# Two handovers of an expert layer moved across stage boundaries: the first gathers of routed rows, the gathers of expert output rows, and the wait for the last expert stores

## The reference

```python
g_gate, g_sel = lax.top_k(softmax(h @ w_group_router + b), 1)      # one of 4 groups
e_gate, e_sel = lax.top_k(softmax(e_logits of that group), 2)      # two of its 8 experts
...
def block_fn(args):                     # one block of 128 slots, one expert
    tok, wt, e = args
    xb = h_pad[tok]
    hidden = silu(xb @ w_gate[e]) * (xb @ w_up[e])
    return (hidden @ w_down[e]) * wt[:, None]
...
out = zeros.at[slot_token].add(y)       # x = x + out, then the final norm, then the second block
```

## Time and profile before

| what | value |
|---|---|
| runs of the kernel before | 3213.03, 3213.64, 3274.13 us |
| median | 3213.64 us |
| span of the profiled execution, first to last instruction | 3215.9 us (its own time outside the profile isn't given) |
| busy shares of the span | PE 94%, DVE 62%, ACT 49%, POOL 15% |
| granted TensorE clock, mean of the span | 0.966 |
| routing stage | about 895 to 924 us of the span |
| experts stage | about 924 to 1399 us |
| mixer tokens stage | about 1399 to 1484 us |

### The profile page before, as it was taken

The page is one execution under the profiler, slowest core; times in us unless marked ns, Lnnn a source line. Parts: engine busy times, 40 slices in busy tenths (PEclk is TensorE's granted clock), DMA queues, the critical chain, the costliest instruction groups (busy, mean ns, idle before and its releaser), DMA issues. The chain is left out here.

```text
span 3215.9 us, 40654 instructions
## 1 busy us (share of the span) xinstructions
PE 3010.4 (94%) x14913; PEld 2476.3 (77%) x14913; DVE 1980.3 (62%) x2873; ACT 1566.4 (49%) x2494; POOL 489.4 (15%) x429
## 2 busy tenths in 40 slices
PE   7998999898969999959999999989999899999999
PEld 6766999686858888858677787777877778888887
DVE  4336888523668888863442434565576576666685
ACT  4225787533548888843521444344453333223443
POOL 0001210000133333220000111113300032222000
PEclk9999999899979999979999999999999999999999
DMA  3334221302168888762242433377764233333653
GB/s 113 90 121 118 60 60 31 114 28 96 66 231 297 296 286 299 249 208 81 77 137 89 120 101 104 108 229 211 208 230 157 73 91 98 103 115 123 226 159 112
DMA packets 299781, 459.71 MB, mean 143 GB/s; under 512 B 47799, under 2 KB 195326, under 8 KB 287042
## 3 DMA queue, kind: packets, MB, share of 16 engines
q1 hardware_dynamic: 274946, 411.72, 40.1%
q10 hardware_dynamic: 9088, 28.58, 2.3%
q0 software_dynamic: 15552, 16.82, 1.8%
HBM read 401.47 MB, written 118.98 MB: 162 GB/s over the span
## 5 line engine op out<-in xcount | busy, mean ns | idle before, releaser
L2866 DVE TENSOR_TENSOR moe_wgu_low<-moe_raw,moe_wgu_high 128x2048 fp32r<-128x2048 f32 x92 | 206.7, 2288 | 45.5 <-ACT moe_wgu_high L2802 39.0
L234 PE MATMUL ga_gate<-second_h_high,ga_ws_high 128*128 128x512 f32 x448 | 197.9, 442 | 12.0 <-DVE ga_ws_low L4202 9.8
L2802 ACT ACTIVATE moe_wgu_high<-moe_raw 128x2048 fp32r<-128x2048 f32 x92 | 171.2, 1909 | 20.2 <-ACT moe_y L2811 20.2
L236 PE MATMUL ga_gate<-second_h_high,ga_ws_low 128*128 128x512 f32 x448 | 180.5, 403 | 0.0
L235 PE MATMUL ga_gate<-second_h_low,ga_ws_high 128*128 128x512 f32 x448 | 179.7, 401 | 0.0
L234 PE MATMUL pr_acc<-second_h_high,pr_ws_high 128*128 128x512 f32 x336 | 138.6, 412 | 12.9 <-DVE pr_stage L3252 9.8
L234 PE MATMUL up_bank<-second_h_high,up_w_high 128*128 128x512 f32 x352 | 139.1, 395 | 9.0 <-DVE up_w_low L3533 7.3
L2971 POOL DMA_INDIRECT moe_rows<-scratch_ffn_rows,slot_of_block x47 | 110.7, 2356 | 226.1 <-PE moe_turned L2755 159.0
L235 PE MATMUL up_bank<-second_h_low,up_w_high 128*128 128x512 f32 x352 | 138.6, 394 | 0.0
L236 PE MATMUL up_bank<-second_h_high,up_w_low 128*128 128x512 f32 x352 | 138.4, 393 | 0.0
L236 PE MATMUL pr_acc<-second_h_high,pr_ws_low 128*128 128x512 f32 x336 | 132.3, 394 | 0.0
(11 more groups left out here) (672 smaller groups left out, 8628.1 us busy)
## 6 DMA issues: line engine op xcount, KB each, us to landing
moe_raw<-in_w_expert_gate_dram SPq DMA_DIRECT2D x32, 1024.0 KB, 4.9
moe_raw<-in_w_expert_up_dram SPq DMA_DIRECT2D x32, 1024.0 KB, 7.4
moe_raw_down<-in_w_expert_down_dram SPq DMA_DIRECT2D x32, 1024.0 KB, 5.9
scratch_gates<-ga_stage SPq DMA_DIRECT2D x96, 256.0 KB, 2.5
scratch_expert_rows<-moe_y ACTq DMA_DIRECT2D x46, 512.0 KB, 4.5
ga_w<-in_w_in_dram SPq DMA_DIRECT2D x92, 256.0 KB, 3.7
scratch_hidden<-X SPq DMA_DIRECT2D x77, 256.0 KB, 2.1
down_rows<-scratch_hidden SPq DMA_DIRECT2D x73, 256.0 KB, 3.1
```

The costliest lines, as they stand in the source:

```text
L234: nc.tensor.matmul(out, w[0], x[0], start=start, stop=False)
L236: return nc.tensor.matmul(out, w[1], x[0], start=False, stop=stop)
L2802: nc.scalar.activation(wgu[i % 2][0][:, :, m, :], raw[(2 * i + m) % RAW][:].rearrange("p (c n) -> p c n", n=FF), ACT.Copy).then_inc(up_hig ...
L2866: nc.vector.tensor_tensor(wgu[i % 2][1][:, :, m, :], raw[(2 * i + m) % RAW][:].rearrange("p (c n) -> p c n", n=FF), wgu[i % 2][0][:, :, m, ...
```

## The change

Four things are edited.

First, at the boundary between routing and experts: POOL's first two gathers (with the wait for `slotted`) leave `route` and stand at the head of POOL's list in `run_experts`, behind the barrier; no semaphore guards them but the barrier. DVE's two `first_low` splits leave `route` too and stand at the head of DVE's list in `run_experts` as `split_up(0, 0)` and `split_up(0, 1)`, behind a wait for `first_gathers`, which POOL raises when it has queued the gathers. Second, in `route` DVE's six instructions for `slots` and `spare_rows` now stand ahead of the wait for the table.

Third, at the boundary between experts and mixer tokens: POOL's waits for the stores and the two gathers of the first tile's output rows leave `run_experts` and stand at the head of POOL's list in `mixer_tokens`; the wait for them before the second tile's gathers is gone, so that four gathers are issued one behind the other. Fourth, the last three stores (block 45, and the two halves of block 46) raise a semaphore that lives through the program, `last_expert_rows_out`. ACT no longer waits for stores at the end of the experts. The next stage waits for this semaphore in two places: POOL ahead of the first gather, and DVE ahead of the low part of weight chunk 2.

```diff
--- before.py
+++ after.py
@@ route
-            pool.wait_ge(made, 15)
-            pool.wait_ge(slotted, 1)
-            for i in range(2):
-                gather_rows(k, rows, slot_of_block, i)
-            pool.sem_inc(gathers, 1)
...
-            dve.wait_ge(tabled, 1)
-            link(v.tensor_scalar(empty[:], table[:, 0:N_BLOCKS], 0.0, NO_TOKEN, ALU.is_equal, ALU.mult))
-            v.scalar_tensor_tensor(slot_of_block[:], table[:, 0:N_BLOCKS], -1.0, empty[:], ALU.add, ALU.add).then_inc(slotted, 1)
-            dve.wait_ge(gathers, 1)
-            first_low(0)
-            first_low(1)
             for c in range(2):
                 link(v.tensor_copy(slots[c][:], slot_f[:, c * ST:(c + 1) * ST]))
...
             link(v.tensor_copy(spare_rows[:], expert_f[:]))
+            dve.wait_ge(tabled, 1)
+            link(v.tensor_scalar(empty[:], table[:, 0:N_BLOCKS], 0.0, NO_TOKEN, ALU.is_equal, ALU.mult))
+            link(v.scalar_tensor_tensor(slot_of_block[:], table[:, 0:N_BLOCKS], -1.0, empty[:], ALU.add, ALU.add))
@@ run_experts
-            sp.dma_start(y_out[SEQUENCE[N - 1]][:, HALF:], y[(N - 1) % 2][:, HALF:]).then_inc(tail_stored, 16)
+            sp.dma_start(y_out[SEQUENCE[N - 1]][:, HALF:], y[(N - 1) % 2][:, HALF:]).then_inc(k.last_expert_rows_out, 16)
...
+            for i in range(2):
+                gather_rows(k, rows, slot_of_block, i)
+            pool.sem_inc(first_gathers, 1)
             for i in range(N):
...
-            pool.wait_ge(ups, N)
-            pool.wait_ge(stored0, 16 * ((N + 1) // 2))
-            pool.wait_ge(stored1, 16 * (N // 2))
-            pool.wait_ge(tail_stored, 16)
-            for c in range(2):
-                gather_outputs(k, slots, c, 0, ahead[2][c])
...
-                act.dma_start(y_out[SEQUENCE[i]][:, cols], y[i % 2][:, cols]).then_inc(stored[i % 2], 16)
+                kept = stored[i % 2] if i + 2 < N else k.last_expert_rows_out
+                act.dma_start(y_out[SEQUENCE[i]][:, cols], y[i % 2][:, cols]).then_inc(kept, 16)
...
             store(N - 1)
-            act.wait_ge(stored0, 16 * ((N + 1) // 2))
-            act.wait_ge(stored1, 16 * (N // 2))
...
+            dve.wait_ge(first_gathers, 1)
+            split_up(0, 0)
+            split_up(0, 1)
             x_low(0)
@@ mixer_tokens
+            pool.wait_ge(k.last_expert_rows_out, 48)
             for t in range(ST):
...
-                if t == 1:
-                    pool.wait_ge(gathered[0], 32)
                 if t >= 2:
                     pool.wait_ge(added, 2 * (t - 2) + 2)
                 for c in range(2):
-                    if t:
-                        gather_outputs(k, slots, c, t, rows[c][t % 2])
+                    gather_outputs(k, slots, c, t, rows[c][t % 2])
...
             for c in range(4):
+                if c == 2:
+                    dve.wait_ge(k.last_expert_rows_out, 48)
                 weight(c)
```

More of the change, by code:

```diff
@@ L165, in __init__ @@
         self.down_in = ctx.enter_context(nc.semaphore("down_in"))
+        self.last_expert_rows_out = ctx.enter_context(nc.semaphore("last_expert_rows_out"))
         self.raw_in = [ctx.enter_context(nc.semaphore(f"expert_weights_in{s}")) for s in range(RAW + RAW_DOWN)]
@@ L2466, in route @@
         table = k.ps("route_table", [P, N_BLOCKS + 1], ctx)
-        made, rounded, shifted, exped, hot_made, ranked, blocks_made, tokens_made, lanes_made, tabled, slotted, gathers = k.sems(
-            "route", "made rounded shifted exped hot_made ranked blocks_made tokens_made lanes_made tabled slotted gathers")
+        made, rounded, shifted, exped, hot_made, ranked, blocks_made, tokens_made, lanes_made, tabled = k.sems(
+            "route", "made rounded shifted exped hot_made ranked blocks_made tokens_made lanes_made tabled")
         block = ctx.enter_context(nc.Block())
@@ L2608, in _ @@
                                 ALU.is_equal).then_inc(lanes_made, 1)
-            def first_low(m):
-                dve.wait_ge(k.expert_highs, m + 1)
-                v.tensor_tensor(first_up[1][:, :, m, :], raw[m][:].rearrange("p (c n) -> p c n", n=FF),
-                                first_up[0][:, :, m, :], ALU.subtract).then_inc(k.expert_lows, 1)
-            dve.wait_ge(tabled, 1)
-            link(v.tensor_scalar(empty[:], table[:, 0:N_BLOCKS], 0.0, NO_TOKEN, ALU.is_equal, ALU.mult))
-            v.scalar_tensor_tensor(slot_of_block[:], table[:, 0:N_BLOCKS], -1.0, empty[:], ALU.add, ALU.add).then_inc(slotted, 1)
-            dve.wait_ge(gathers, 1)
-            first_low(0)
-            first_low(1)
             for c in range(2):
@@ L2663, in run_experts @@
         (turns, x_highs, x_lows, ups, silus, hiddens, h_turns, h_highs, h_lows, down_highs, down_lows,
-         downs, y_ready, stored0, stored1, tail_copied, tail_stored) = k.sems(
+         downs, y_ready, stored0, stored1, tail_copied, first_gathers) = k.sems(
             "moe", "turns x_highs x_lows ups silus hiddens h_turns h_highs h_lows down_highs down_lows "
-            "downs y_ready stored0 stored1 tail_copied tail_stored")
+            "downs y_ready stored0 stored1 tail_copied first_gathers")
         stored, up_highs, up_lows = (stored0, stored1), k.expert_highs, k.expert_lows
```

## The result

The changed kernel took 3201.03 us (median of 19 runs, 3194.35 to 3211.02) against 3213.03 us for the kernel before (19 runs beside them): a ratio of 0.995 with a 95% interval of 0.9935 to 0.9966. By the medians it is 12.0 us faster, where 9.5 us were forecast; by the ratio of 0.995 it is about 16 us, by its interval 11 to 21 us. The profiled execution took 3198.80 us and spans 3197.0 us, 18.9 us less than the one before.

The account below looks back on a forecast made before the run. PE was taken to bound the experts and mixer tokens, with barrier holes held by DVE at the first boundary and POOL at the second. 3213.6 minus 2.4 plus 7.1, 9.5 us, gave 3204.1 us; range 3199 to 3210.5 us.

Parts of the forecast that it names:

- First boundary, 2.4 us: Routing to experts: PE turns the first gathered rows at 921.8 instead of 924.25, a gain of 2.4 us.
- Second boundary, 7.1 us: Experts to mixer tokens: DVE adds the first tile's rows at 1395.95 instead of 1403.05, a gain of 7.1 us.
- one slow issue, 0.6 us: Experts to mixer tokens: DVE's subtractions beside POOL slow one gather issue, so the second gather lands 0.6 us later.
- What is late next: Mixer tokens: second tile's rows, needed 5.7 us after the first's, come in time; weight chunk 4 has two us left.
- First rival: Experts to mixer tokens: four gathers share DMA engines, first rows land 4 us later; 3208.1 us, chance 0.12.
- Second rival: Experts to mixer tokens: POOL's 8.4 us are its passage to the next stage and recur behind the barrier; 3210.5 us, chance 0.08.
- with gathers in flight: Experts to mixer tokens: POOL, its gathers in flight, reaches the barrier some 8.4 us after its last issue ends.
- At the first boundary it was DVE: Routing to experts: DVE's splits and six small instructions, ending at 923.55, held the barrier; PE started 0.70 us later.
- Third rival: Mixer tokens: clock stays at half through the stage, 31 us more, kernel ends at 3235 us; chance 0.04.
- A first gather behind either boundary more than 2 us after the other engines' start: Both boundaries: a sign listed as showing the forecast wrong, if the gap exceeded 2 us.
- 2.4 plus 7.1 is 9.5: Whole kernel: the two boundary gains sum to 9.5 us, giving 3204.1 us.
- Far under the 2% that a measurement of this kernel can tell: Whole kernel: the forecast gain of 0.3% cannot be told from no change; chance 0.97 of lying within 2%.

Follow-up runs that it names:

- gathers_ahead: The changed kernel, but POOL's first two gathers stand in routing again ahead of the barrier, only DVE's splits stay moved; 3209.44 us (1 run).
- pair_wait: The changed kernel with POOL's old wait between the gathers of the first and second tile given back; 3202.45 us (1 run).
- wait_landed: The kernel before, with POOL also waiting for the first tile's two gathers to land before the barrier ending the experts; 3216.64 us (1 run).
- early_drain: The kernel before plus one POOL drain while idle near the experts' end, ahead of its waits and last two gathers; 3210.07 us (1 run).
- half_drain: The kernel before plus one POOL drain half way through the experts, with 44 DMAs still to come; 3208.87 us (1 run).
- split_sem: The changed kernel with a separate semaphore for the first gather of output rows, so DVE adds them before the second lands; 3199.98 us (12 runs).
- before_again: The kernel before, unchanged, profiled once more for the spread; 3239.63 us (1 run).
- after_again: The changed kernel, unchanged, run and profiled once more for the spread; 3200.15 us (12 runs).
- b_only: The changed kernel with the routing-to-experts boundary as before, so only the experts-to-mixer-tokens edits; 3205.27 us (12 runs), ratio 0.997 to the kernel before.
- a_only: The changed kernel with the experts-to-mixer-tokens boundary as before, so only the routing-to-experts edits; 3211.75 us (12 runs), ratio 1.0002 to the kernel before.

## Why the prediction was right, and where it was wrong

*First boundary, 2.4 us: right, in size and in mechanism.* Routing to first turning fell from 29.49 to 27.06 us. The small instructions are hidden, the splits hide beside the gather. Two parts were off and cancelled: the gather was issued 1.77 us after the row numbers' start (916.57 less 915.39 is 1.18 before), 0.2 us later than the 1.6 taken; and PE had its rows 4.6 us after its issue (912.51 to 917.10), where 4.8 was taken. That they cancelled was luck. The Trainium skill, page "DMA: Bandwidth & Descriptors", section "Anatomy of one DMA — SWDGE (gpsimd) path", gives an estimate of 3.2 us for it. The trace doesn't agree: 4.6 us, nearer to the case's own rows.

*Second boundary, 7.1 us: right mechanism, 0.7 us too small.* The term that was mis-sized is "one slow issue, 0.6 us". From SP's store to the first addition there are now three steps: 2.90 us to POOL's first issue (1375.81 to 1378.71), 1.31 to its second, and 5.84 until that has landed, 10.05 in all. Before they were 3.41, 1.26 and 5.41 us, 10.08 in all, with the barrier behind them. So the slow issue moved the second one by 0.05 us only; a later landing (0.43 us) is made up by an earlier first issue (0.51 us). Why POOL issues earlier wasn't tried; the stores land as before, 2.5 to 2.6 us after their issue, and POOL now passes one wait and not four. The bare barrier, 7.77 us, is what was gained.

*The slow issue.* The row that the 0.6 us rested on, 1.55 us, recurs in every kernel with the old second boundary (1.55, 1.56), but the same subtractions beside the moved issue cost it 0.06 us (1.01 against 0.95). The issue behind it took 1.16 us, which moved no landing that the sum counts. So the subtractions alone don't make it slow. Beside the experts' larger splits an issue is slow: in the routing rows above the second gather's took 1.98 us, in gathers_ahead, where DVE is idle, 1.00. The Trainium skill, page "SBUF — State Buffer", section "Who interferes with whom", would have neither slowed, by what it says of writing descriptors. At the second boundary its answer, 7.7 us, was nearer to the 7.8 measured than mine; at the first boundary the trace speaks against it, 1.98 against 1.00 us.

*What is late next: right.* The second addition starts 5.7 us after the first (1391.58), as forecast; chunk 4 does not hold ACT up. pair_wait shows that this rested on the removed wait, which the prediction took for free: it is worth 3.7 us.

*First rival (the four gathers share the DMA engines): wrong.* It set 4 us; pair_wait shows 0.3 at most.

*Second rival (the hole isn't the gathers'): half true, and its time wrong.* Its premise is what wait_landed, early_drain and half_drain show: the hole is POOL's passage to the barrier and not the landing. Its conclusion, that the passage comes behind the barrier again, does not follow: after the change POOL's last issue in the experts ends 36.8 us before its next (rows above), some 34 us before the others reach the barrier, and nothing is left of its passage to be seen: ACT starts 0.88 us after its last work. The forecast's own wording, "with gathers in flight", had the wrong cause and the right sum. Its evidence "at the first boundary nothing of the kind is seen" was misread, and with it "At the first boundary it was DVE": POOL arrives there too, 4.2 us after its last issue and about when DVE does. It made no difference to the sum, since gathers and splits moved together.

*Third rival (the clock at half through the stage): wrong.* The granted clock in the mixer tokens stage rose from 0.97 to 1.00 (rows by stretch above).

*A sign that could not tell.* "A first gather behind either boundary more than 2 us after the other engines' start" was to show the forecast wrong. It is 2.15 us at the second boundary (1376.56 to 1378.71), but the forecast's own sum has 2.5 us there (1386.1 to 1388.61), since POOL waits for the stores.

*The step that failed: the sum itself, "2.4 plus 7.1 is 9.5".* It holds the two boundaries and nothing more, and put the stages behind them at nothing ("The rest of the chain is unchanged"). In the profiles they were not: beside 2.4 and 7.8 us at the boundaries, the experts took 2.2 us less and the mixer tokens 1.4 us less, with the same instructions. In the trace it is the granted clock. The first 18 us from the first turning, before:

```profile
924.25:942.25 18.00, 15.47 (x59) 12.19 (x60) 10.01 (x9) 11.25 (x11) 5.64 (x4) 0.77 0.40 138
```

And after:

```profile
917.10:935.10 18.00, 15.47 (x63) 12.30 (x64) 10.96 (x10) 11.95 (x11) 6.08 (x5) 0.81 0.44 150
```

At the end of the experts there is one more stretch at half clock, before:

```profile
1376.40:1379.80 3.40, 1.00 (x6) 0.59 (x4) 2.72 (x3) 2.80 (x4) 0.00 (x0) 1.00 0.57 183
1379.80:1383.20 3.40, 3.28 (x8) 2.60 (x9) 0.07 (x1) 0.00 (x0) 0.00 (x0) 0.50 0.38 154
```

The first product behind it, before:

```profile
1379.92 0.79 PE L234 MATMUL moe_down<-moe_down_ws_high,moe_ht_high 128*128 128x512 f32 x1 [2.52 <-DVE moe_ht_low L2882]
```

And after:

```profile
1372.04 0.50 PE L235 MATMUL moe_down<-moe_down_ws_high,moe_ht_high 128*128 128x512 f32 x1 [2.52 <-DVE moe_ht_low L2866]
```

PE had been idle for the same 2.52 us in both; before, the clock went to half (1.2 GHz) behind it and the product took 0.79 us, after it stayed at 2.4 GHz and took 0.50. Those 3.28 us of busy time at half clock are 1.6 of the 2.2 us; the rest is the earlier rise at the start. This stretch is there in five of the six executions with the old first boundary (all but wait_landed) and in none of the six with the splits moved. The like stretch in the mixer tokens stage is in four of the six with the old second boundary and in one of the six with the new (split_sem). Both repeat in before_again, and both are absent in after_again. That is no proof that the change takes them away: the stage ahead of routing, which no kernel here touches, repeats just as well (152.9 us twice before, 148.5 us twice after) and differs between kernels with the same instructions in it, and wait_landed has neither stretch although its experts are those of the kernel before. So they mostly go with the change; whether it causes them, and what makes the clock fall after one such pause and not after another, was not tried and stays open. Counting them, 2.4 + 2.2 + 7.8 + 1.4 is 13.8 us; the boundaries alone are 10.2. The forecast's range had three such stretches as a margin at its lower end, but priced the likeliest case without any.

The other 5.1 us by which the two profiles differ lie outside the stages that the change reaches. Of these 4.4 lie ahead of routing, where before has 152.9 us and after 148.5, at a mean granted clock of 0.95 and 0.98; half_drain and early_drain, with the same instructions there as before, have 148.3 and 148.4 too. The remaining 0.7 us are spread over the other stages.

*The chances.* "Far under the 2% that a measurement of this kernel can tell" was wrong: 19 runs of each kernel give an interval of 0.3% in all. A change of 0.3% to 0.5% was told from none, in after, in b_only and in split_sem; a gain of 0.1%, as in a_only, was not. The median, 3201.0 us, lies in the range, 3.1 us under the forecast; the ratio of 0.995, applied to the 3213.6 us that the forecast started from, would give 3197.6 us, under the range's lower end of 3199. What the two boundaries gave, 10.2 us in the profiles, doesn't reach that far.

## What to carry to other kernels

An engine that issues many DMAs should turn to a stage's barrier early, or be drained while it is idle: its passage was longer the more it had issued since its last drain (or the longer ago that was), and everyone waits for it. Whether a hole at a barrier is in the transfers or in the engine is told by waiting for the transfers first: if the hole grows by the wait, it is the engine. And when a wait is moved across a barrier, the waits between the transfers behind it must be looked at as well, since they then come onto the path (3.7 us here).

## What the runs showed of the hardware

- From the end of POOL's last DMA issue until the next stage starts it takes 8.3 to 8.5 us with 92 DMAs since the last drain, 6.6 us with 44 and 4.2 to 4.5 us with two. With 92 it does not matter whether the last have landed (when POOL first waits for them, 8.0 us still follow); with two the stage starts 0.4 to 0.6 us after the landing.
- Four indirect gathers of 128 rows issued back to back (about 1.3 us apart) delay the first pair by 0.3 us at most against a pair alone (10.05 and 9.8 us against 9.7).
- A pause of PE of 2.52 us was followed by half clock (a product of 0.79 us and not 0.50) in five of the twelve profiles and not in the other seven, with the same instructions around it; the two kernels that were profiled twice gave the same answer both times.
